# One rotary product for two cache pages, in the decoder kernel with a paged cache

## The reference

```python
def expand_kv(latent, w_ukv, k_nope_norm):
    kv = (latent @ w_ukv).reshape(latent.shape[:-1] + (MLA_HEADS, QK_NOPE + V_HEAD))
    return rms_norm(kv[..., :QK_NOPE], k_nope_norm), kv[..., QK_NOPE:]

def attend(q_nope, q_pe, k_nope, k_pe, v, mask):
    s = (jnp.einsum('...qhd,...khd->...hqk', q_nope, k_nope)
         + jnp.einsum('...qhr,...kr->...hqk', q_pe, k_pe)).astype(jnp.float32) * ATTN_SCALE
    p = jax.nn.softmax(jnp.where(mask, s, NEG_INF), axis=-1).astype(v.dtype)
    return jnp.einsum('...hqk,...khd->...qhd', p, v)

# mla_sample, for each of the 8 sequences:
lat = concatenate([cache_lat[layer, pages].reshape(past, KV_LORA), lat_new])
kp = concatenate([cache_kpe[layer, pages].reshape(past, QK_ROPE), kp_new])
k_nope, v = expand_kv(lat, w_ukv, k_nope_norm)
attend(qn, qp, k_nope, kp, v, mask)
```

## Time and profile before

| | |
|---|---|
| Median of 3 runs | 1589.9 us (1588.88 to 1589.93) |
| Profiled execution | 1589.27 us, span 1587.4 us |
| PE busy | 1561.0 us, 98% |
| DVE busy | 1068.7 us, 67% |
| ACT busy | 884.6 us, 56% |
| POOL busy | 521.1 us, 33% |
| TensorE clock granted | 1.00 |
| Page stage | about 140 to 400 us, and 927 to 1190 us |

### The profile page before, as it was taken

The page is one execution under the profiler, slowest core; times in us unless marked ns, Lnnn a source line. Parts: engine busy times, 40 slices in busy tenths (PEclk is TensorE's granted clock), DMA queues, the critical chain, the costliest instruction groups (busy, mean ns, idle before and its releaser), DMA issues.

```text
span 1587.4 us, 33215 instructions
## 1 busy us (share of the span) xinstructions
PE 1561.0 (98%) x10860; PEld 1516.9 (96%) x10860; DVE 1068.7 (67%) x1626; ACT 884.6 (56%) x1612; POOL 521.1 (33%) x659
## 2 busy tenths in 40 slices
PE   7999999999999999999999999999999999999999
PEld 7987999999999999999999789999999999999999
DVE  6787777777664766664376877777775748666633
ACT  5786676767534444443357866666764345444432
POOL 3732377776700000000058213767667001000000
PEclk9999999999999999999999999999999999999999
DMA  7331455553544444444454224655535444444443
GB/s 274 120 108 52 139 183 167 163 161 109 186 134 155 151 147 146 150 155 146 146 188 136 76 73 137 196 152 166 163 111 174 145 154 151 147 146 146 151 152 112
DMA packets 114690, 232.90 MB, mean 147 GB/s; under 512 B 12881, under 2 KB 78706, under 8 KB 114450
## 3 DMA queue, kind: packets, MB, share of 16 engines
q1 hardware_dynamic: 112178, 223.13, 45.3%
q0 software_dynamic: 2400, 8.36, 1.6%
HBM read 228.98 MB, written 2.46 MB: 146 GB/s over the span
## 4 chain that ended last, share of the span: by engine, by line
PE 90%; DVE 4%; ACT 2%; DVEq 1%; issue 1%; ACTq 1%; DMA 0%; POOL 0%; SPq 0%; POOLq 0%
PE PS L803 53%; PE PS L1048 26%; PE PS L1081 2%; PE PS L1082 2%; DVE w_lo L1742 1%; PE PS L1043 1%; ACT w_hi L1297 1%; DVEq L1736 1%; PE PS L830 1%; PE PS L859 1%; ACTq L1301 0%; ACT r_hi L1297 0%; PE PS L937 0%; ACTq L1485 0%; DMA x<-in_xT 0%
## 5 line engine op out<-in xcount | busy, mean ns | idle before, releaser
L1742 DVE TENSOR_TENSOR w_lo<-raw,w_hi 128x1024 fp32r<-128x1024 f32 x258 | 325.0, 1261 | 222.9 <-ACT w_hi L1297 220.0
L1297 ACT ACTIVATE w_hi<-raw 128x1024 fp32r<-128x1024 f32 x258 | 272.3, 1057 | 347.3 <-PE PS L803 333.1
L803 PE MATMUL PS<-h_hi,w_hi 128*128 128x320 f32 x1360 | 426.4, 314 | 11.1 <-DVE h_lo L1769 10.3
L803 PE MATMUL PS<-h_hi,w_lo 128*128 128x320 f32 x1360 | 421.3, 310 | 0.0
L803 PE MATMUL PS<-h_lo,w_hi 128*128 128x320 f32 x1360 | 421.3, 310 | 0.0
L803 PEld LDWEIGHTS PS<-h_hi,w_hi 128*128 128x128 f32 x1360 | 256.3, 188 | 14.2 <-issue 9.5
L803 PEld LDWEIGHTS PS<-h_lo,w_hi 128*128 128x128 f32 x1360 | 256.4, 189 | 0.9
L803 PEld LDWEIGHTS PS<-h_hi,w_lo 128*128 128x128 f32 x1360 | 256.2, 188 | 0.0
L1048 PE MATMUL PS<-comb_hi,lt_hi 128*128 128x288 f32 x1024 | 239.9, 315 | 0.0
L1297 ACT ACTIVATE ksqp<-PS 128x512 f32<-128x512 f32 x256 | 153.2, 598 | 152.4 <-PE PS L1048 150.3
L2097 DVE TENSOR_REDUCE kss<-ksqp 128x8 f32<-128x512 f32 x256 | 174.2, 682 | 85.3 <-ACT ksqp L1297 84.2
(11 more groups left out here) (317 smaller groups left out, 2662.0 us busy)
## 6 DMA issues: line engine op xcount, KB each, us to landing
raw<-in_stream SPq DMA_DIRECT2D x258, 512.0 KB, 3.5
tpage<-in_tcache SPq DMA_DIRECT2D x256, 192.0 KB, 2.4
rrow<-in_rcache SPq DMA_DIRECT2D x256, 128.0 KB, 2.6
x<-in_xT SPq DMA_DIRECT2D x2, 640.0 KB, 6.9
sbias<-in_sbias POOLq DMA_DIRECT2D x2, 640.0 KB, 6.2
out_yT<-x SPq DMA_DIRECT2D x4, 320.0 KB, 2.2
const<-in_consts SPq DMA_DIRECT2D x1, 1088.0 KB
wgate<-in_wgate POOLq DMA_DIRECT2D x2, 512.0 KB, 4.5
```

Source lines behind the costliest of these rows:

```text
L803: done = mm(out, w[:, slot, c], a, start=first and n == 0 and m == 0, stop=last and n == len(pairs) - 1 and m == 2)
L1297: return nc.scalar.activation(out, in_, func, **kw)
L1742: V.tensor_tensor(w_lo[:, s, :], raw[:, s, :], f(w_hi[:, s, :]), ALU.subtract).then_inc(lo_done.sem, 1)
```

## The change

Two pages share their tiles. A stationary tile of 128 columns no longer holds the 128 tokens of one page, but half v (64 tokens) of the first page and half v of the second. A page in `tcache` now has 5 groups of 64 columns: four for the latent (dimension half, token half), and one for rotary, whose 128 rows are twice (token half, 32 dimensions). The pair's rotary tile has 128 columns: 64 of each page. The moving operand `q_rot` has 256 columns in two groups of 128: the queries' high part, and their low part; in each group 64 columns have only the rows of token half 0, and 64 only those of half 1, the rest being zero (`half` is a 0/1 mask). One product per pair, ahead of the odd page's keys, gives a high and a low group; VectorE adds the two with a reduction out of PSUM and writes `srot` in SBUF, which `finished_scores` adds in.

GpSimd makes `q_rot` in `queries` with three more operations. `rotary_spread_lo` goes, and `q128` is plain float32. The rotary results alternate between banks 6 and 5, and the sequence's small products use bank 4 always; TensorE waits for all eight banks ahead of the first sequence. `rrow` gets the same tokens: a page's two halves go to two slots, on 64 partitions.

```diff
-    tpage = sb("tpage", [128, TBUF, CHUNK, 384], on=st4)
-    lt_hi = sb("lt_hi", [128, 2, CHUNK, 384], f32r, on=st4)
+    tpage = sb("tpage", [128, TBUF, CHUNK, 5, 64], on=st4)
+    q_rot = sb("q_rot", [128, 2, 2, 2 * HT], f32r, on=st4)
+    lt_hi = sb("lt_hi", [128, 2, 5, CHUNK * 64], f32r, on=st4)
...
-                sp.dma_start(rrow[:, (2 * m + i) % RRAW, :],
-                             ins["rcache"][bass.ds(l * NPHYS + at[i], 1)].rearrange("o p n -> p (o n)")
+                sp.dma_start(rrow[64 * i:64 * i + 64, 2 * m % RRAW:2 * m % RRAW + 2, :],
+                             ins["rcache"][bass.ds(l * NPHYS + at[i], 1)].rearrange("o (v r) n -> (o r) v n", v=2)
...
+            pool.wait_ge(q128_ready.sem, q128_ready.at(l, 1))
...
+                half = cst("half").rearrange("p (v o) -> p v o", o=1).to_broadcast([128, 2, HT])
+                both = q128[:, bass.ds(b, 1), :].to_broadcast([128, 2, HT])
+                hi_ = q_rot[:, par, 0].rearrange("p (v c) -> p v c", v=2)
+                lo_ = q_rot[:, par, 1].rearrange("p (v c) -> p v c", v=2)
+                nc.gpsimd.tensor_tensor(hi_, both, half, ALU.mult)
...
+                nc.gpsimd.tensor_tensor(lo_, both, f(hi_), ALU.subtract)
+                pool.drain()
+                nc.gpsimd.tensor_tensor(lo_, f(lo_), half, ALU.mult).then_inc(qc.sem, 1)
...
-                half = lt_hi[64:128, c % 2, :, 256:384]
+                half = lt_hi[64:128, c % 2, 4].rearrange("p (i c) -> p i c", i=CHUNK)
                 pool.drain()
-                nc.gpsimd.tensor_tensor(half, tpage[64:128, c % TBUF, :, 256:384], f(half), ALU.subtract).then_inc(pt_rope.sem, 1)
+                nc.gpsimd.tensor_tensor(half, tpage[64:128, c % TBUF, :, 4], f(half), ALU.subtract).then_inc(pt_rope.sem, 1)
...
+        def rotary_scores(l, b, c, par):
+
+            pe.wait_ge(pt_rope.sem, pt_rope.at(l, b * NCH + (c + 1)))
+            if not (isinstance(b, int) and b == 0 and c < 2):
+                pe.wait_ge(rot_added.sem, rot_added.at(l, b * NCH + (c - 1)))
+            mm(PS[:, 6 - c % 2, 0:4 * HT], lt_hi[:, c % 2, 4], q_rot[:, par].rearrange("p s c -> p (s c)"),
+               start=True, stop=True)
...
-            r0 = HT * (p % (NPG // 2))
-            mm(PS[:, rotary_bank(p, par), r0:r0 + HT], lt_hi[:, t, i, 256:384], q128_of(b), start=True, stop=True)
+            if i == 1:
+                rotary_scores(l, b, p // CHUNK, par)
...
-                        last = mm(PS[:, 2 * s + g, c0:c0 + 288], a[:, t, i, 128 * k:128 * k + 128], w[:, k, g, c0:c0 + 288],
+                        last = mm(PS[:, 2 * s + g, c0:c0 + 288], a[:, t, 2 * k + i], w[:, k, g, c0:c0 + 288],
...
-            for b in (0, 1, 2, 3, 4, 6, 7):
+            for b in range(8):
                 pe.wait_ge(bank_free[b].sem, banks.last(l, b))
...
-            A(lt_hi[:, c % 2], tpage[:, c % TBUF], ACT.Copy).then_inc(pt_hi.sem, 1)
+            A(lt_hi[:, c % 2].rearrange("p j (i c) -> p i j c", i=CHUNK), tpage[:, c % TBUF], ACT.Copy).then_inc(pt_hi.sem, 1)
...
-            into = sraw[:, par, at].rearrange("p a c -> p (a c)")
-            last = V.tensor_tensor(into, into, PS[:, bank, :], ALU.add)
-            last.then_inc(s_rot.sem, 1)
+            V.tensor_tensor(sraw[:, par, at], sraw[:, par, at], srot[:, par, at], ALU.add)
+
+        def rotary_scores(l, b, c, par):
+
+            V.tensor_reduce(srot[:, par, 2 * c:2 * c + 2].rearrange("p v c -> p (v c)"),
+                            PS[:, 6 - c % 2, 0:4 * HT].rearrange("p (s x) -> p x s", s=2), AX.X, ALU.add).then_inc(rot_added.sem, 1)
...
                 dve.wait_ge(pk_sq.sem, pk_sq.at(l, b * NPG + (p + 1)))
                 V.tensor_reduce(kss[:, par, p, :], ksqp[:, s, :].rearrange("p (h c) -> p h c", h=H), AX.X, ALU.add).then_inc(pk_ss.sem, 1)
+                if p % CHUNK == 1:
+                    rotary_scores(l, b, p // CHUNK, par)
```

More of the change, by code:

```diff
@@ L184, in build_program @@
     rrow = sb("rrow", [128, RRAW, KVL], on=st4)
-    beside_rows = sb("beside_rows", [128, 768], on=st4)
-    lt_lo = sb("lt_lo", [128, 2, CHUNK, 256], f32r, on=st4)
-    r_hi, r_lo = sb("r_hi", [128, RROWS, ROW], f32r, on=st4), sb("r_lo", [128, RROWS, KVL], f32r, on=st4)
+    r_lo = sb("r_lo", [128, RROWS, KVL], f32r, on=st4)
+    beside_rows = sb("beside_rows", [128, 256], on=st4)
+    lt_lo = sb("lt_lo", [128, 2, 4, CHUNK * 64], f32r, on=st4)
+    r_hi = sb("r_hi", [128, RROWS, ROW], f32r, on=st4)
+    srot = sb("srot", [128, 2, NPG, HT], on=st4)
     st4.close()
@@ L1128, in pages @@
         def pages(l):
-            for b in (0, 1, 2, 3, 4, 6, 7):
+            for b in range(8):
                 pe.wait_ge(bank_free[b].sem, banks.last(l, b))
             pe.wait_ge(latnew_ready.sem, latnew_ready.at(l, 2))
-            pe.wait_ge(q128_ready.sem, q128_ready.at(l, 2))
             sequence(l, 0, 0, tail=False, values=False, older=False)
-            pe.wait_ge(bank_free[5].sem, banks.last(l, 5))
             sequence(l, 1, 1, values=False, older=False)
@@ L1520, in spatial_and_attention_inputs @@
                          PS[:, 6, :].rearrange("p (h j b t) -> p h j b t", h=4, j=2, b=NB)[:, :, jt], ACT.Copy)
-            last.then_inc(q128_hi.sem, 1)
+            last.then_inc(q128_ready.sem, 1)
+            release(6)
         def prompt_attention(l):
@@ L1926, in spatial_and_attention_inputs @@
             lo(y0_lo[:], ti[:], y0_hi[:]).then_inc(y0_ready.sem, 1)
-        def rotary_spread_lo(l, jt):
-            dve.wait_ge(q128_hi.sem, q128_hi.at(l, 1))
-            for r in (1, 3):
-                rows = slice(32 * r, 32 * r + 32)
-                dst = q128[rows, :, 32 * jt:32 * jt + 32].rearrange("p b (h t) -> p h b t", h=4)
-                src = PS[rows, 6, :].rearrange("p (h j b t) -> p h j b t", h=4, j=2, b=NB)[:, :, jt]
-                last = V.tensor_tensor(dst, src, f(dst), ALU.subtract)
-            last.then_inc(q128_ready.sem, 1)
         def new_latent_lo(l):
@@ L1979, in prompt_attention @@
             normalised(0)
-            rotary_spread_lo(l, 0)
-            rotary_spread_lo(l, 1)
-            release(6)
             dve.wait_ge(sn_mm.sem, sn_mm.at(l, 1))
@@ L2025, in pages_lo @@
             dve.wait_ge(pt_hi.sem, pt_hi.at(l, b * NCH + (c + 1)))
-            lo(lt_lo[:, c % 2], tpage[:, c % TBUF, :, 0:256], lt_hi[:, c % 2, :, 0:256]).then_inc(pt_lo.sem, 1)
+            lo(lt_lo[:, c % 2].rearrange("p j (i c) -> p j i c", i=CHUNK), tpage[:, c % TBUF, :, 0:4].rearrange("p i j c -> p j i c"),
+               lt_hi[:, c % 2, 0:4].rearrange("p j (i c) -> p j i c", i=CHUNK)).then_inc(pt_lo.sem, 1)
         def finished_scores(l, b, par, second):
@@ L2032, in finished_scores @@
             half = NPG // 2
-            at, bank = (slice(half, NPG), 6) if second else (slice(0, half), 4 + par)
+            at = slice(half, NPG) if second else slice(0, half)
             inv = kss[:, par, at].rearrange("p a (h o) -> p a h o", o=1).to_broadcast([128, half, H, NT])
@@ L2108, in sequence @@
                 if older and p == 9:
-                    keep(l, b - 3, 5 - par)
+                    keep(l, b - 3, 4)
                 if tail and p == 9:
@@ L2368, in _constants @@
     c["fold"] = np.tile(np.eye(64), (2, 2))
+    c["half"] = np.tile(np.repeat(np.eye(2), 32, 0), (2, 1))
     return np.concatenate([c[n] for n in CONST], 1).astype(np.float32)
@@ L2403, in _layout @@
         "page_table": p["page_table"].reshape(1, -1),
-        "tcache": by_dim.reshape(DEPTH * NPHYS, 128, 384),
+        "tcache": by_dim,
         "rcache": lat,
```

72 lines of the change are left out of this document (32 added, 40 removed).

## The result

The changed kernel is slower: 1604.61 us median (1603.34 to 1609.81) against 1589.91 (1588.88 to 1590.38) for the kernel before, measured beside it, ratio 1.0099, 95% interval 1.0081 to 1.0117. The forecast was 1582.2, range 1576 to 1590. The profiled execution took 1603.65 us, 14.4 more than that of before.

The account below looks back on a forecast made before the run. TensorE was taken to bound the page stage, until VectorE's lt_lo comes too late. TensorE -14.0, start +1.7 and VectorE's waits +4.6 sum to -7.7 us, so 1582.2 us, range 1576 to 1590.

Parts of the forecast that it names:

- TensorE, -14.0 us: Page stage: 128 rotary products of 256 columns at 0.12 us replace 256 of 64 columns at 0.115, -14.0 us.
- The start, +1.7: Page stage's start: TensorE waits for all eight banks, the fourth y_lo, 0.84 us later, twice, +1.7 us.
- The reduction, R = 0.43: VectorE, per page pair: new reduction out of PSUM costs R = 0.43 us start to start, ends 0.33 and 1.24.
- 0.12 more for each of two adds ahead of page 8: VectorE: adds of the rotary part, now with both operands in SBUF, cost 0.12 us more each (812 against 688 ns).
- The relief, 0.27: GpSimd's shorter low part of the rotary rows gives back half of a long lt_lo's extra 0.54 us: 0.27.
- The sum: Whole kernel: -14.0 + 1.7 + 4.6 = -7.7 us, from TensorE's products, the stage's start and VectorE's waits.
- the forecast's own formula: Slack of lt_lo at page 8, less reduction, TensorE's earlier arrival and two adds: 0.59 - 0.43 - 0.11 - 0.24 = -0.19 us.
- The slower one: Rival: VectorE's reduction pays per output, R = 1.24, making lt_lo late at page 12; +18 us, 1608; chance 0.12.
- That VectorE hides it all: Rival: relief from GpSimd's shorter work is as large as VectorE's reductions; -12.3 us, 1577.6; chance 0.28.

Follow-up runs that it names:

- experiment 2: Changed kernel with the product of scores and norms written to PSUM, so the addition reads one operand there: 1599.29 us; with the addition left out instead: 1586.81 us.
- experiment 1: Kernel before, with only the addition's second operand taken from SBUF (other half of the scores) instead of PSUM: 1618.04 us, ratio 1.0182.
- experiment 3: Changed kernel, with bank 5 waited for at page 3 of sequence 0 instead of at the page stage's start: 1602.60 us, ratio 1.0075.

## Why the prediction was wrong

- **TensorE, -14.0 us: right.** 13.6 by the pair without r_lo.
- **The start, +1.7: right.** TensorE is idle 1.44 us in front of the first key product, where it was idle 0.74 in front of the first rotary product before; 0.70 twice is 1.4.
- **The reduction, R = 0.43: too dear.** It is 0.33, the end without a penalty for the stride. Line 2051, from which I took one, reads SBUF; this one reads PSUM, and takes 412 ns like the unstrided line 1964. The Trainium skill's penalty for leaving a line ("SBUF — State Buffer", "Door 1: The DMA port swizzle") is stated there for SBUF's 16-byte lines; the prediction carried it over to a PSUM read by VectorE, and this read, whose two summed elements lie 512 bytes apart, shows none.
- **The additions, "0.12 more for each of two adds ahead of page 8": the step that failed.** The mean is 0.57 more (1258 against 688 ns), and ahead of page 8 in sequence 5 it is 0.84 for each: 1.68 us where the sum had 0.24. I took the mean of line 2036 as the price of two SBUF operands. But that mean (812) mixes 20 instructions of about 0.68 us, no dearer than the addition from PSUM, with 12 of 0.95 to 1.25, and each of the twelve began inside an lt_hi of GpSimd (its low part of the rotary rows, line 711). Two of these lt_hi, before, in sequence 5:

```profile
305.31 0.73 POOL L711 TENSOR_TENSOR lt_hi<-tpage,lt_hi 64x256 fp32r<-64x256 f32 x1 [0.16 <-issue]
...
312.68 1.05 POOL L711 TENSOR_TENSOR lt_hi<-tpage,lt_hi 64x256 fp32r<-64x256 f32 x1 [0.49 <-ACT lt_hi L1297]
```

They end at 306.04 and 313.73; the product of 305.63 ends at 306.59 and the lt_lo of 313.04 at 314.27, 0.55 and 0.54 later. So the price is nothing or the rest of a GpSimd instruction, by where the two fall against each other. The prediction named this exclusion and still charged a mean; the additions stand where the longest of these instructions, r_lo, runs.
- **The relief, 0.27: came, and was taken back.** GpSimd's lt_hi went from 925 to 600 ns, more than forecast, and the lt_lo that was held for 1.23 us takes 0.69 in the changed kernel (sequence 5, the split for page 10). But ahead of it VectorE's scaling of the summed values (olat, 0.41 us at 311.93 before) now begins inside an r_lo, takes 1.20, and ends 0.15 after it; its mean over 16 went from 508 to 966 ns. The sum had no term for that:

```profile
314.82 1.20 POOL L750 TENSOR_TENSOR r_lo<-rrow,r_hi 128x512 fp32r<-128x512 f32 x1 [0.32 <-issue]
314.97 1.20 DVE L2076 TENSOR_SCALAR olat<-olat,linv 128x256 f32<-128x256 f32 x1
316.87 0.69 DVE L1752 TENSOR_TENSOR lt_lo<-tpage,lt_hi 128x512 fp32r<-128x512 f32 x1
```

- **The sum.** With the measured sizes the forecast's own formula gives for page 8: 0.59 - 0.33 - 0.11 - 2 x 0.84 = -1.53 us; measured is a wait of 1.64. (The lt_lo itself takes 0.88, as it began inside another GpSimd instruction; with its 0.19 the formula gives -1.72.) From the first page's first key product to the last page's, the stage went from 250.1 and 251.0 us to 257.4 and 257.6, +13.9: if 14 us came off TensorE's work, about 28 us of standing were put on. The lt_lo row shows 23.0 of it, because a wait is counted from the modelled end of the product ahead: at page 8 of sequence 5 the starts are 1.93 apart (311.50 to 313.43) where 0.12 is usual, which is 1.81 for a wait row of 1.64. As an estimate, 0.17 for each of the 28 waits is 4.8 more, 27.8 in all.
- **The rivals.** The slower one had the wait (lt_lo) and nearly the time (1608), and that is luck: its reason was wrong, since 128 outputs cost nothing extra (412 ns), and its place was page 12, where 3.0 us stand against 16.5 at page 8. That VectorE hides it all is refuted by 23.0 us.

## What to carry to other kernels

When an operand moves from PSUM to SBUF on VectorE, don't price it by a group's mean: look for GpSimd's long instructions that read SBUF, and charge each meeting with what is left of them. A meeting avoided can move to the next VectorE instruction with two SBUF operands (experiment 2), so it pays only where that one has slack. And free time in the mean is no protection: before the change VectorE was idle for 8 us of each sequence (32.90 against 24.86), and in the changed kernel it still set the time, because its long instructions stood packed ahead of the one that TensorE waits for.

## What was not expected of the hardware

- In some places TensorE's granted clock fell to 1.2 GHz behind a wait, for some 3 us, and the spacing of products went from 0.26 to 0.48. With two reductions it fell behind four of the eight waits of 2.34 to 2.53 us and stayed at 1.00 behind the other four. It fell behind both waits of 1.89 us of experiment 1 and behind one of 1.83 in experiment 3, and stayed at 1.00 behind all ten waits of 1.42 to 1.84 at page 8 of the changed kernel. Where it fell, that cost 1.8 us more (36.7 against 34.9 us): a second price of waiting, which does not come every time. What decides it is open.
- GpSimd's subtraction of 128x512 elements took 1.32 us in one instruction, 4 x 0.52 in four, 2 x 0.81 in two.
- In the page stages of the changed kernel 62 of VectorE's products, additions and lt_lo (lines 2032, 2034 and 1752) took over 0.75 us. Every one of them began inside a GpSimd instruction and ended 0.54 to 0.56 us after it, whichever instruction it was (r_lo, lt_hi or p_hl). In the kernel before, all 57 of that kind (lines 2036 and 1745) did the same.
